# Experts' gated values turned four blocks at a time, kept in the place of the last norm's row

## The chip, the cores and the metric

The kernel runs on one core of one Trainium2 chip. The metric is the device time of one execution in microseconds; less is better. The core's engines are TensorE (PE; its weight loads PEld), VectorE (DVE), ScalarE (ACT), GpSimd (POOL) and SyncE (SP). Each runs its own instruction stream, and they meet at semaphores. A "q" behind an engine's name (PEldq, DVEq) is its sequencer: branches, waits, counts.

## What is computed

Two transformer blocks over 256 tokens of width 1024. The part that the change touches is the end of the second block: a mixture of experts (eight experts, two per token, 2816 hidden values) with the closing layer norm.

```python
def moe_swiglu(x, w_router, b_router, w_in, w_out):
    ...
    def expert_block(args):
        xb, e = args
        h = xb @ w_in[e]
        return (jax.nn.silu(h[:, :D_FF]) * h[:, D_FF:]) @ w_out[e]
...
def layer_norm(x, g, b):
    xf = x.astype(jnp.float32)
    mu = jnp.mean(xf, axis=-1, keepdims=True)
    var = jnp.mean(jnp.square(xf - mu), axis=-1, keepdims=True)
    return ((xf - mu) * lax.rsqrt(var + LN_EPS) * g + b).astype(x.dtype)
...
        x = layer_norm(DN_ALPHA * x + ffn, ln_ffn_g[i], ln_ffn_b[i])
```

## The kernel before

All engines run the same plan: first block, sparse feed-forward of the first block, first layer of the second block, second layer with the router, then the experts. The experts are one body (`expert`), run in a loop for experts 0 to 6, written out for expert 7, and written out three more times as overflow blocks (`OVER`), each in an `If` on a count from the router; where an expert has no more than 128 tokens the `Else` (`skip`) runs instead and only raises the semaphores by what the body would have raised (`each_expert`, L714). With the inputs used, all three overflow blocks are skipped.

One expert, for its 128 token slots: the weights stream through a ring of six units of 2 MB. 11 units are slabs of the up product ("up"; each gives 256 columns of each half), 7 are pieces of the output product ("y"). A unit is used in two halves ("pieces"). Each piece is split by ScalarE into a rounded part (`piece_hi`, four places, L1192) and by VectorE into the rest (`weights_low`, L2222), and TensorE multiplies hi*hi, hi*low and low*hi. The order in which TensorE works is the list `Y`, that of ScalarE and VectorE the list `E_SEQ` (L365 to L379).

Between up and y stand the gated values. ScalarE takes the silu of half a bank into `silu_e` (L1216), VectorE multiplies it by the other half into `gated` (L2258), which has two places in the scratch region; TensorE turns a slab's 128x256 values by two 128x128 transposes into a bank (L1632); ScalarE copies them rounded to `ge_hi` (L1192), VectorE subtracts to `ge_low` (L2234). This job is called ("ge", n), one for each of the 11 slabs, and stands in both lists behind slab n + 2. VectorE waits before it writes slab n's gated values until ("ge", n - 2) is turned. The tokens of the next expert are fetched by POOL with an indirect DMA into `tokens`, the first of two places of `rows` (L610, L868), and turned four blocks at a time (L1584).

`rows` has two places of 1024 values on all partitions. The norms' rows (g and b) are loaded into them in turn, even ones into place 0, odd ones into place 1 (`load_row`, L810 to L815). Of the last norm's two rows, b (`late_row + 1`, place 1) is loaded before the experts begin (L864), because place 1 is then free; g (`late_row`, place 0) is loaded after the last tokens are turned (L869, L870).

At the end VectorE adds each expert's sums to the tokens (L2272), goes through its three skips (L2280), and normalises tile 0, then tile 1 (`layer_norm_tile`, L1726): statistics, a multiplication by g (L1731), the root, the reciprocal (L1733), and two halves with b (L1736). SP writes the outputs by halves as they are ready (L801). `layer_norm_tile` waits for both rows ahead of L1731.

The semaphore `e_product` counts TensorE's jobs of the experts: it is raised by one at the end of each, and by a whole expert's number, `N_EP`, by TensorE's `skip`:

```python
        def skip(b):
            pe.wait_ge(e_product, b * N_EP + N_EP)
            pe.sem_inc(e_product, N_EP)
```

The other names that the diff touches: `E_BANK` gives each job its PSUM bank; `wait_split(..., e_low, what, ...)` waits until VectorE has the low part of `what`; `e_freed["vector"]` counts what VectorE has read or written.

Of the kernel before, what the change touches and what calls it, by code (L numbers as in the profile page):

```python
# [21 lines left out]
P = 128  # L22
S, D = 256, 1024
# [236 lines left out]
def two_blocks(nc, a):  # L260
# [101 lines left out]


    HIS = 4
    Y, E_SEQ = [], []  # L365
    for i in range(N_PIECE):
        Y.append(piece_end(i))
        n, more = i // 2, [("piece", i + HIS)] if i + HIS < N_PIECE else []
        turned = ("ge", n - 2) if i % 2 and 2 <= n < N_UP + 2 else None
        if i < 2 * N_UP and i % 2:  # L370
            E_SEQ += [("up", n), ("piece", i + HIS - 1)]
        if i >= 2 * N_UP or i % 2:
            E_SEQ += more
        if turned:
            Y.append(turned)
            E_SEQ.append(turned)
        if turned == ("ge", 1):
            Y.append(SLOTS)
            E_SEQ.append(SLOTS)  # L379
    E_ORDER = {False: Y[:-1] + GATHERED[:1] + Y[-1:] + GATHERED[1:] + SUMS + [("pickT", 0)], True: GATHERED + [("pickT", 0)] + Y + SUMS}  # L380
# [115 lines left out]
    top[0] = N_HI + 2 * FC * P + TILES * P + 2 * D  # L496
    pick = area(TILES * P, P)
    slot_gate = area(1)
    silu_e, gated = area(2 * S, S), area(2 * S, S)
    logits, r_mask, r_first, r_hot = (area(TILES * NE, NE) for _ in range(4))  # L500
    r_gate, r_slot = (area(TILES * (NE + 1), NE + 1) for _ in range(2))
    r_top, r_idx, r_idxf = area(TILES * 8, 8), area(TILES * 8, 8, U32), area(TILES * 8, 8)
# [164 lines left out]
    E_BANK = {("pickT", 0): 6, SLOTS: 7}  # L667
    for n in range(N_UP):
        E_BANK["up", n] = n % 4
        E_BANK["ge", n] = 4 + n % 2  # L670
    for n in range(N_SUM):
        E_BANK["sum", n] = n
    for h in range(HALVES):
# [131 lines left out]
    @block.gpsimd  # L805
    def _(pool):
        own = Own(pool, pool_step)
        pool.dma_start(pos_i, a["positions"][0].partition_broadcast(P)).then_inc(pos_in, 16)

        def load_row(i):  # L810
            if i >= 2:
                pool.wait_ge(row_used, i - 1)
            name = rows_order[i]
            src = a[name[0]][name[1]] if isinstance(name, tuple) else (a[name] if name == "g_final" else a[name][0])
            pool.dma_start(rows[:, i % 2, :], src.partition_broadcast(P)).then_inc(row_in[i % 2], 16)  # L815

        for i in range(2, 4):
            load_row(i)

        pool.wait_ge(product_ready, pl.nth["in", N_IN - 1])  # L820
        pool.dma_start(x_tok[:, :, :], a["x"][0].rearrange("(t p) n -> p t n", p=P)).then_inc(x_again, 16)
        pool.wait_ge(merged, KD)
        pool.dma_start(mem2T[:, :, :], a["mem_2_T"].rearrange("(k p) s -> p k s", p=P)).then_inc(mem2_in, 16)
        pool.dma_start(pos_i, a["positions_2"][0].partition_broadcast(P)).then_inc(pos_in, 16)


        def gather_u(s, k):
            if k == 0:
                pool.wait_ge(search_done, s + 1)
            pool.wait_ge(dots_done, s * TOPK + k + 1)  # L830
            pool.indirect_dma_start(u_ring[:, k % UV, :], None, a["peer_u"][0],  # L831
                                    bass.IndirectOffsetOnAxis(idx[:, s % IDX_SETS, k:k + 1], 0)).then_inc(u_in[k % UV], 16)

        def gather_v(s, k):
            n = s * TOPK + k
            if n < VV and n % (UNIT // D) == 0:
                pool.wait_ge(product_ready, pl.nth[V_FROM[n // (UNIT // D)]])
            if n < VV or by_pe(n - VV):
                pool.wait_ge(v_used, summed_to(n - VV))
            else:  # L840
                pool.wait_ge(v_added, ADDED.index(n - VV) + 1)
            pool.indirect_dma_start(v_row(n), None, a["peer_v"][0],  # L842
                                    bass.IndirectOffsetOnAxis(idx[:, s % IDX_SETS, k:k + 1], 0)).then_inc(v_in[n % VV], 16)

        def u_rows_ahead(n):
            return TOPK if n < UNIT // D else TOPK + 8 if n < 2 * UNIT // D else TOPK + 4

        gathered_u = 0
        for n in range(STEPS * TOPK):
            while gathered_u < min(n + 1 + u_rows_ahead(n), STEPS * TOPK):  # L850
                gather_u(gathered_u // TOPK, gathered_u % TOPK)
                gathered_u += 1
            gather_v(n // TOPK, n % TOPK)
        late_row = len(rows_order) - 2
        assert late_row % 2 == 0
        for i in range(4, late_row):
            load_row(i)
        pool.wait_ge(cum_ready, 1)
        for h in range(SH):
            row = other_half[h % 2].start  # L860
            pool.dma_start(kz[row:row + 1, h, :], f_cum[h:h + 1, :]).then_inc(decay_rows_in, 16)
        pool.wait_ge(normed, HALVES * TILES * 7)
        pool.dma_start(x_rows.rearrange("(t p) n -> p t n", p=P), x_tok[:, :, :]).then_inc(x_saved, 16)
        load_row(late_row + 1)  # L864
        pool.wait_ge(x_saved, 16)
        for b in range(NE - 1):
            pool.wait_ge(slots_ready, b + 1)
            pool.indirect_dma_start(tokens, None, x_rows, bass.IndirectOffsetOnAxis(slot_token[:, 0:1], 0)).then_inc(tokens_in, 16)  # L868
        pool.wait_ge(e_product, (NE - 1) * N_EP + e_at(GATHERED[-1], False) + 1)  # L869
        load_row(late_row)  # L870


    @block.scalar
    def _(act):
# [298 lines left out]
        def split(what, b, over):  # L1173

            kind, n = what
            if kind == "y":
                act.wait_ge(e_freed["scalar"], (b + 1 + over) * e_n["scalar"])
                act.activation(ye_hi[:, 512 * n:512 * n + 512], wait_e(what, b, over), ACT.Copy, scale=slot_gate).then_inc(e_hi, 1)
                return
            if kind == "gather":  # L1180
                src, dst = wait_e(what, b, over).rearrange("p (k s) -> p k s", k=4), xe_hi[:, 4 * n:4 * n + 4, :]
            elif kind == "ge":
                src, dst = wait_e(what, b, over)[:, 0:S].rearrange("p (f s) -> p f s", f=2), ge_hi[:, 2 * n:2 * n + 2, :]
            else:
                src, dst = piece(n), hi_of(n)
                if n % 2 == 0:
                    u = n // 2
                    turn = b if over or n >= HIS else b + 1
                    act.wait_ge(weight_in[u % RING], turn * per_expert[u % RING] + pl.loaded[u % RING] + e_loaded[u])
                if n >= HIS or not over:  # L1190
                    act.wait_ge(e_product, b * N_EP + N_EP + e_at(piece_end((n - HIS) % N_PIECE), over) + 1)
            act.activation(dst, src, ACT.Copy).then_inc(e_hi, 1)  # L1192
# [60 lines left out]
    def _(pe):  # L1253
# [355 lines left out]
        def expert(e, b, over):  # L1609
# [5 lines left out]
            for j in Y:  # L1615
# [11 lines left out]
                if j[0] == "ge":  # L1627
                    n = j[1]
                    bank = bank_of(j, b, over)
                    pe.wait_ge(e_freed["vector"], b * e_n["vector"] + e_n["vector"] + e_nth(("up", n), over))  # L1630
                    for f in range(2):
                        ins = pe.transpose(bank[:, f * P:(f + 1) * P], gated[:, n % 2, f * P:(f + 1) * P], ident)  # L1632
                    ins.then_inc(e_product, 1)
                    continue
                i = next(i for i in range(N_PIECE) if piece_end(i) == j)
# [12 lines left out]
                else:  # L1648
                    o, h = divmod(i - 2 * N_UP, HALVES)
                    bank = bank_of(("y", h), b, over) if o == 0 else psum[:, E_BANK["y", h], :]  # L1650
                    f0 = sum(OUT_ROWS[:o])
                    wait_split(pe, e_low, ("ge", (f0 + OUT_ROWS[o] - 1) // 2), b, over)
                    wait_split(pe, e_low, ("piece", i), b, over)
                    for k in range(OUT_ROWS[o]):
                        f = f0 + k
# [33 lines left out]
    def _(dve):  # L1689
# [36 lines left out]
        def layer_norm_tile(t, src):  # L1726

            own(dve.bn_aggr(mv[:, 2 * t:2 * t + 2], bn[:, 12 * t:12 * t + 12]))  # L1728
            tell(dve.tensor_scalar(stat[:, t:t + 1], mv[:, 2 * t + 1:2 * t + 2], LN_EPS, None, ALU.add), square_ready, n_square)  # L1729
            g, b = wait_row(dve, n_row[0]), wait_row(dve, n_row[0] + 1)  # L1730
            own(dve.scalar_tensor_tensor(x_tok[:, t, :], src[:, t, :], mv[:, 2 * t:2 * t + 1], g, ALU.subtract, ALU.mult))  # L1731
            dve.wait_ge(root_ready, n_square[0])
            own(dve.reciprocal(rstd[:, t:t + 1], rstd[:, t:t + 1]))  # L1733
            for h in range(HALVES):
# [482 lines left out]
        def split(what, b, over):  # L2217
# [12 lines left out]
            if kind == "gather":  # L2230
                bank, hi, low = psum[:, E_BANK[what], :].rearrange("p (k s) -> p k s", k=4), xe_hi[:, 4 * n:4 * n + 4, :], xe_low[:, 4 * n:4 * n + 4, :]
            else:
                bank, hi, low = psum[:, E_BANK[what], 0:S].rearrange("p (f s) -> p f s", f=2), ge_hi[:, 2 * n:2 * n + 2, :], ge_low[:, 2 * n:2 * n + 2, :]
            dve.tensor_tensor(low, bank, hi.bitcast(F32), ALU.subtract).then_inc(e_low, 1)  # L2234
            dve.wait_ge(e_low, b * N_SPLIT + N_SPLIT + E_SPLITS[over].index(what) + 1)
            dve.sem_inc(e_freed["vector"], 1)
# [1 line left out]
        def expert(e, b, over):  # L2238
# [4 lines left out]
            for j in E_SEQ:  # L2243
# [9 lines left out]
                    continue  # L2253
                n = j[1]
                dve.wait_ge(e_silu, b * N_UP + n + 1)
                if n >= 2:
                    wait_e(("ge", n - 2), b, over)
                dve.tensor_tensor(gated[:, n % 2, :], silu_e[:, n % 2, :], psum[:, E_BANK[j], S:2 * S], ALU.mult)\  # L2258
                   .then_inc(e_freed["vector"], 1)
            last = b == NE - 1 if isinstance(b, int) else False  # L2260
            for j in E_OUT if over else OPENING + CLOSING:
# [115 lines left out]
```

## Time and profile before

| | |
|---|---|
| median of 3 runs | 2350.22 us (2348.09 to 2350.32) |
| profiled execution, its own time | 2348.31 us |
| its span | 2346.3 us |
| TensorE busy | 2129.1 us, 91% |
| VectorE busy | 1563.8 us, 67% |
| ScalarE busy | 1069.1 us, 46% |
| POOL busy | 512.2 us, 22% |
| granted TensorE clock, mean | 0.990 |

The span goes from the first to the last instruction; the time of the execution has some 2 us more around it. The experts take about the last third of the span. In the rows further on, a time is counted from the start of the span; an instruction's duration on TensorE is longer than the distance to the next one, since products overlap.

### The profile page before, as it was taken

To read this page: it belongs to the slowest core of one execution; us is meant where nothing else is said; L and a number is where in the kernel's file an instruction comes from. 1 tells how busy PE (TensorE), PEld (TensorE's weight loads), DVE (VectorE), ACT (ScalarE), POOL (GpSimd) and SP (SyncE) were. 2 spreads that over 40 slices of the span, in tenths; PEclk is the share of its full clock that TensorE was granted. 3 is DMA by queue.
4 is the path that set the end of the run, shared out by engine and by line. 5 is a ranking of instruction groups with operands and counts; after the bars stand their busy time and mean duration, and the time that the engine had idled before them with its cause. 6 is when DMAs were issued, how large, how long until landed. Compare 5 with 4: busy or idle time off the path is not lost. (4 is left out here: it accounts for less than half of the span.)

```text
span 2346.3 us, 27245 instructions
## 1 busy us (share of the span) xinstructions
PE 2129.1 (91%) x9328; PEld 1529.5 (65%) x9328; DVE 1563.8 (67%) x2560; ACT 1069.1 (46%) x1565; POOL 512.2 (22%) x550
## 2 busy tenths in 40 slices
PE   7999999877777777789999999899999999999997
PEld 5998867322222222257599886578878788787875
DVE  5775338666666666544455432479888898888987
ACT  3496014221222212114444325367777777777764
POOL 0000007777777777610000010000000000000000
PEclk9999999999999999999999999999999999999998
DMA  8444429999999999994253643279999999999993
GB/s 309 159 156 180 163 92 378 404 410 409 409 409 409 409 410 409 409 351 160 90 180 135 242 162 108 99 241 318 363 344 355 350 360 362 344 359 350 357 363 136
DMA packets 356585, 683.41 MB, mean 291 GB/s; under 512 B 14016, under 2 KB 222016, under 8 KB 356352
## 3 DMA queue, kind: packets, MB, share of 16 engines
q1 hardware_dynamic: 279008, 401.24, 50.4%
q0 software_dynamic: 77472, 280.80, 30.2%
q8 instruction: 61, 1.00, 0.2%
q14 instruction: 44, 0.36, 0.0%
HBM read 679.88 MB, written 2.10 MB: 291 GB/s over the span
## 5 line engine op out<-in xcount | busy, mean ns | idle before, releaser
L2222 DVE TENSOR_TENSOR weights_low<-weight_ring,piece_hi 128x2048 fp32r<-128x2048 f32 (+1 forms) x286 | 590.1, 2109 | 48.6 <-ACT piece_hi L1192 42.7
L1440 PE MATMUL psum<-weight_ring,region 128*128 128x512 f32 x988 | 478.0, 609 | 142.8 <-DMA weight_ring<-in_peer_v,region 139.6
L1192 ACT ACTIVATE piece_hi<-weight_ring 128x2048 fp32r<-128x2048 f32 (+1 forms) x286 | 494.7, 1768 | 30.4 <-PE psum L1658 27.8
L1440 PEld LDWEIGHTS psum<-weight_ring,region 128*128 128x128 f32 x988 | 169.0, 189 | 451.4 <-issue 303.5
L2041 DVE CUSTOM_DVE_ANT_0 weight_ring<-weight_ring,psum 128x1024 f32<-128x1024 f32 x224 | 273.6, 1221 | 206.0 <-DMA weight_ring<-in_peer_u,region 206.0
L1645 PE MATMUL psum<-piece_hi,tokens_hi 128*128 128x512 f32 x704 | 284.7, 404 | 5.4 <-DVE weights_low L2222 2.7
L831 POOL DMA_INDIRECT weight_ring<-in_peer_u,region x256 | 248.0, 969 | 140.0 <-DVE region L2015 53.0
L1647 PE MATMUL psum<-piece_hi,tokens_low 128*128 128x512 f32 x704 | 277.8, 395 | 0.0
L1646 PE MATMUL psum<-weights_low,tokens_hi 128*128 128x512 f32 x704 | 277.7, 394 | 0.0
L842 POOL DMA_INDIRECT weight_ring<-in_peer_v,region x256 | 242.5, 947 | 90.7 <-issue 69.7
L1043 ACT ACTIVATE region<-constants,region 128x128 f32<-128x128 f32 x247 | 88.3, 395 | 284.6 <-PE psum L1440 209.6
L1291 PE MATMUL psum<-actT,weight_ring 128*128 128x256 f32 x720 | 161.5, 384 | 1.8 <-DMA weight_ring<-in_w_mem_kv 1.8
L1645 PEld LDWEIGHTS psum<-piece_hi,tokens_hi 128*128 128x128 f32 x704 | 132.6, 188 | 36.7 <-DVE weights_low L2222 5.8
L1647 PEld LDWEIGHTS psum<-piece_hi,tokens_low 128*128 128x128 f32 x704 | 132.5, 188 | 31.2
L1291 PEld LDWEIGHTS psum<-actT,weight_ring 128*128 128x128 f32 x720 | 138.4, 193 | 21.8 <-DMA weight_ring<-in_w_mem_kv 2.2
L1646 PEld LDWEIGHTS psum<-weights_low,tokens_hi 128*128 128x128 f32 x704 | 132.8, 189 | 27.8
L868 POOL DMA_INDIRECT rows<-x_rows,region x7 | 6.6, 946 | 641.6 <-DVE region L2247 641.6
L1656 PE MATMUL psum<-piece_hi,gated_hi 128*128 128x512 f32 x352 | 140.3, 399 | 0.3 <-PEq L1570 0.3
L1658 PE MATMUL psum<-piece_hi,gated_low 128*128 128x512 f32 x352 | 137.6, 391 | 0.0
L1657 PE MATMUL psum<-weights_low,gated_hi 128*128 128x512 f32 x352 | 137.1, 389 | 0.0
L890 ACT ACTIVATE region<-psum 128x256 f32<-128x256 f32 (+2 forms) x119 | 56.1, 475 | 173.9 <-PE psum L1291 89.2
L2123 DVE TENSOR_TENSOR ring_low<-weight_ring,ring_hi 128x2048 fp32r<-128x2048 f32 (+1 forms) x36 | 76.0, 2114 | 58.5 <-ACT ring_hi L1085 58.5
(313 smaller groups left out, 3434.0 us busy)
## 6 DMA issues: line engine op xcount, KB each, us to landing
weight_ring<-in_w_exp_in SPq DMA_DIRECT2D x176, 1024.0 KB, 11.8
weight_ring<-in_w_exp_out SPq DMA_DIRECT2D x48, 1536.0 KB, 9.3
weight_ring<-in_w_in SPq DMA_DIRECT2D x12, 2048.0 KB, 7.8
weight_ring<-in_w_ffn_in SPq DMA_DIRECT2D x22, 1024.0 KB, 7.7
weight_ring<-in_w_exp_out SPq DMA_DIRECT2D x8, 2048.0 KB, 8.9
weight_ring<-in_w_out SPq DMA_DIRECT2D x6, 2048.0 KB, 8.4
weight_ring<-in_w_in_fox SPq DMA_DIRECT2D x5, 2048.0 KB, 7.9
weight_ring<-in_w_ffn_out SPq DMA_DIRECT2D x6, 1536.0 KB, 6.7
```

Of the source, the lines that this page charges most:

```text
L831: pool.indirect_dma_start(u_ring[:, k % UV, :], None, a["peer_u"][0], bass.IndirectOffsetOnAxis(idx[:, s % IDX_SETS, k:k + 1], 0)).then_in ...
L842: pool.indirect_dma_start(v_row(n), None, a["peer_v"][0], bass.IndirectOffsetOnAxis(idx[:, s % IDX_SETS, k:k + 1], 0)).then_inc(v_in[n % V ...
L1192: act.activation(dst, src, ACT.Copy).then_inc(e_hi, 1)
L1291: ins = pe.matmul(bank[:, 0:S], w[:, k, c * P:(c + 1) * P], src[:, k, :], start=(k == 0), stop=(k == nk - 1))
L1440: ins = pe.matmul(psum[:, peer_bank(t, half), :], diag[:, k, :], v_row(n)[:, 512 * half:512 * half + 512], start=(s < TILES and k == 0), s ...
L1645: pe.matmul(bank, xe_hi[:, k, :], h_, start=(k == 0), stop=False)
L1646: pe.matmul(bank, xe_hi[:, k, :], l_, start=False, stop=False)
L1647: ins = pe.matmul(bank, xe_low[:, k, :], h_, start=False, stop=(k == KD - 1))
L1656: pe.matmul(bank, ge_hi[:, f, :], hi[:, k, :], start=(f == 0), stop=False)
L1658: ins = pe.matmul(bank, ge_low[:, f, :], hi[:, k, :], start=False, stop=(f == FC - 1))
L2041: dve.tensor_tensor_reduce(u_ring[:, k % UV, :], u_ring[:, k % UV, :], h2, 1.0, 0.0, ALU.mult, ALU.add, u_dot[:, t, k:k + 1]).then_inc(dot ...
L2222: dve.tensor_tensor(low_of(n), piece(n), hi_of(n).bitcast(F32), ALU.subtract).then_inc(e_low, 1)
```

## The change

`ge` jobs become fewer and larger: job q turns slabs 2q and 2q + 1 with four transposes into one bank; the last one has the single slab 10. There are six (`N_TURN`). Job q stands behind slab 2q + 3, the last behind slab 12 of the list (the second unit of the output product), where ("ge", 10) stood. The copy to `ge_hi` and the subtraction to `ge_low` take 512 columns at once. `gated` gets four places instead of two, and these are place 1 of `rows`. So row b of the last norm can't be loaded ahead of the experts: POOL loads it after all experts and overflow blocks are counted in `e_product`. `layer_norm_tile` waits for b only after the multiplication by g.

```diff
     HIS = 4
+    N_TURN = -(-N_UP // 2)
+    TURNED_AT = {2 * q + 3: ("ge", q) for q in range(N_TURN - 1)}
+    TURNED_AT[N_UP + 1] = ("ge", N_TURN - 1)
+    units_turned = lambda q: range(2 * q, min(2 * q + 2, N_UP))
...
-        turned = ("ge", n - 2) if i % 2 and 2 <= n < N_UP + 2 else None
+        turned = TURNED_AT.get(n) if i % 2 else None
...
-        if turned == ("ge", 1):
+        if turned == ("ge", 0):
...
-    silu_e, gated = area(2 * S, S), area(2 * S, S)
+    silu_e = area(2 * S, S)
+    gated = rows[:, 1, :].rearrange("p (u s) -> p u s", u=4)
...
-        E_BANK["ge", n] = 4 + n % 2
+    for q in range(N_TURN):
+        E_BANK["ge", q] = 4 + q % 2
...
         pool.dma_start(x_rows.rearrange("(t p) n -> p t n", p=P), x_tok[:, :, :]).then_inc(x_saved, 16)
-        load_row(late_row + 1)
+        pool.wait_ge(row_used, late_row)
         pool.wait_ge(x_saved, 16)
...
         pool.wait_ge(e_product, (NE - 1) * N_EP + e_at(GATHERED[-1], False) + 1)
         load_row(late_row)
+        pool.wait_ge(e_product, (NE + OVER + 1) * N_EP)
+        load_row(late_row + 1)
...
-                src, dst = wait_e(what, b, over)[:, 0:S].rearrange("p (f s) -> p f s", f=2), ge_hi[:, 2 * n:2 * n + 2, :]
+                f0, nf = 4 * n, 2 * len(units_turned(n))
+                src, dst = wait_e(what, b, over)[:, 0:nf * P].rearrange("p (f s) -> p f s", f=nf), ge_hi[:, f0:f0 + nf, :]
...
-                    pe.wait_ge(e_freed["vector"], b * e_n["vector"] + e_n["vector"] + e_nth(("up", n), over))
-                    for f in range(2):
-                        ins = pe.transpose(bank[:, f * P:(f + 1) * P], gated[:, n % 2, f * P:(f + 1) * P], ident)
+                    pe.wait_ge(e_freed["vector"], b * e_n["vector"] + e_n["vector"] + e_nth(("up", units_turned(n)[-1]), over))
+                    for u in units_turned(n):
+                        for f in range(2):
+                            at = (2 * (u % 2) + f) * P
+                            ins = pe.transpose(bank[:, at:at + P], gated[:, u % 4, f * P:(f + 1) * P], ident)
...
-            g, b = wait_row(dve, n_row[0]), wait_row(dve, n_row[0] + 1)
+            g = wait_row(dve, n_row[0])
             own(dve.scalar_tensor_tensor(x_tok[:, t, :], src[:, t, :], mv[:, 2 * t:2 * t + 1], g, ALU.subtract, ALU.mult))
+            b = wait_row(dve, n_row[0] + 1)
...
-                if n >= 2:
-                    wait_e(("ge", n - 2), b, over)
-                dve.tensor_tensor(gated[:, n % 2, :], silu_e[:, n % 2, :], psum[:, E_BANK[j], S:2 * S], ALU.mult)\
+                if n >= 4:
+                    wait_e(("ge", (n - 4) // 2), b, over)
+                dve.tensor_tensor(gated[:, n % 4, :], silu_e[:, n % 2, :], psum[:, E_BANK[j], S:2 * S], ALU.mult)\
```

## Rows read from the trace of the kernel before

**Rows 1.** Busy time by stretch: us, then PE, PEld, DVE, ACT, POOL, clock, DMA.

```profile
1600.00:2200.00 600.00, 595.60 (x2688) 482.00 (x2688) 533.67 (x431) 436.35 (x395) 5.64 (x6) 1.00 1.05 353
2300.00:2346.00 46.00, 29.04 (x127) 22.77 (x125) 33.24 (x36) 18.29 (x17) 0.00 (x0) 0.86 0.24 85
```

**Rows 2.** Waits, 1600 to 2200: waiting line, releaser, us in total, times, longest.

```profile
PEld psum L1645 <- DVE weights_low L2222: 4.9, 6, 0.8
PEld psum L1668 <- DVE out_low L2225: 3.8, 6, 0.6
```

**Rows 3.** Groups by form, 1600 to 2200: busy us, mean ns, idle before.

```profile
L2234 DVE TENSOR_TENSOR gated_low<-psum,gated_hi 128x256 fp32r<-128x256 f32 x67 | 28.1, 419 | 0.0
L1192 ACT ACTIVATE gated_hi<-psum 128x256 fp32r<-128x256 f32 x67 | 24.8, 371 | 0.0
L2234 DVE TENSOR_TENSOR tokens_low<-psum,tokens_hi 128x512 fp32r<-128x512 f32 x12 | 8.3, 692 | 2.7 <-DVE out_low L2225 2.7
L1192 ACT ACTIVATE tokens_hi<-psum 128x512 fp32r<-128x512 f32 x12 | 7.1, 590 | 0.0
```

**Rows 4.** Timeline of TensorE around a turn of two: start, us.

```profile
1699.93 0.39 PE L1647 MATMUL psum<-piece_hi,tokens_low 128*128 128x512 f32 x1
1700.16 0.38 PE L1632 MATMUL psum<-constants,region 128*128 128x128 f32 x2
1700.30 0.48 PE L1656 MATMUL psum<-piece_hi,gated_hi 128*128 128x512 f32 x1
1700.61 0.40 PE L1657 MATMUL psum<-weights_low,gated_hi 128*128 128x512 f32 x1
```

**Rows 5.** Timeline of TensorE around a turn of four (tokens).

```profile
1728.18 0.60 PE L1584 MATMUL psum<-constants,rows 128*128 128x128 f32 x4
1728.54 0.48 PE L1656 MATMUL psum<-piece_hi,gated_hi 128*128 128x512 f32 x1
1728.85 0.40 PE L1657 MATMUL psum<-weights_low,gated_hi 128*128 128x512 f32 x1
```

**Rows 6.** Timeline: two low parts, and the product that needs the first.

```profile
1784.50 4.49 DVE L2222 TENSOR_TENSOR weights_low<-weight_ring,piece_hi 128x2048 fp32r<-128x2048 f32 x2 [0.23 <-ACT piece_hi L1192]
...
1787.93 0.48 PE L1645 MATMUL psum<-piece_hi,tokens_hi 128*128 128x512 f32 x1
```

**Rows 7.** Lines L723 and L1678: ns min/median/max, first and last start.

```profile
L723 ACTq COMPARE_BRANCH  x3: 45/45/50, 2328.1 to 2331.2; - x3
L723 PEldq COMPARE_BRANCH  x3: 3899/5022/5420, 2330.1 to 2339.4; - x3
...
L1678 PEldq EVENT_SEMAPHORE  x3: 51/51/51, 2334.0 to 2344.9; - x3
```

**Rows 8.** Timeline: POOL's load of row g, and what released it.

```profile
2227.28 0.60 PE L1584 MATMUL psum<-constants,rows 128*128 128x128 f32 x4
...
2228.18 0.57 POOL L815 DMA_DIRECT2D rows<-in_ln_ffn_g  x1 [64.25 <-PE psum L1584]
```

**Rows 9.** Lines L815 (at 1358, at 2228) and L801: the issues, us to landing.

```profile
L815 POOL DMA_DIRECT2D rows<-in_ln_attn_g x1: 528/528/528, 1358.5 to 1358.5; - x1
DMA to landing us min/median/max: 3.7/3.7/3.7
...
L815 POOL DMA_DIRECT2D rows<-in_ln_ffn_g x1: 567/567/567, 2228.2 to 2228.2; - x1
DMA to landing us min/median/max: 6.6/6.6/6.6
...
L801 SPq DMA_DIRECT2D out<-x_tok x4: 332/342/360, 2338.4 to 2343.8; - x4
DMA to landing us min/median/max: 2.0/2.0/5.4
```

**Rows 10.** The tail: VectorE's timeline in tile 0, POOL's drain (ns).

```profile
2336.14 1.29 DVE L1731 SCALAR_TENSOR_TENSOR x_tok<-work_tok,small,rows 128x1024 f32<-128x1024 f32 x1
2337.46 0.16 DVE L1733 RECIPROCAL small<-small 128x1 f32<-128x1 f32 x1
...
L2314 POOLq DRAIN  x1: 10397/10397/10397, 2228.2 to 2228.2; - x1
```

More of the change, by code:

```diff
@@ L854, in _ @@
         late_row = len(rows_order) - 2
-        assert late_row % 2 == 0
         for i in range(4, late_row):
@@ L1651, in expert @@
                     f0 = sum(OUT_ROWS[:o])
-                    wait_split(pe, e_low, ("ge", (f0 + OUT_ROWS[o] - 1) // 2), b, over)
+                    wait_split(pe, e_low, ("ge", (f0 + OUT_ROWS[o] - 1) // 4), b, over)
                     wait_split(pe, e_low, ("piece", i), b, over)
@@ L2232, in split @@
             else:
-                bank, hi, low = psum[:, E_BANK[what], 0:S].rearrange("p (f s) -> p f s", f=2), ge_hi[:, 2 * n:2 * n + 2, :], ge_low[:, 2 * n:2 * n + 2, :]
+                f0, nf = 4 * n, 2 * len(units_turned(n))
+                bank, hi, low = psum[:, E_BANK[what], 0:nf * P].rearrange("p (f s) -> p f s", f=nf), ge_hi[:, f0:f0 + nf, :], ge_low[:, f0:f0 + nf, :]
             dve.tensor_tensor(low, bank, hi.bitcast(F32), ALU.subtract).then_inc(e_low, 1)
```

## Prediction

> **What bounds the kernel now.** I read the busy time by stretch first. From 1600 to 2200 us, inside the expert loop, TensorE is busy 595.6 of 600 us, VectorE 533.7, ScalarE 436.4, all at full granted clock [rows 1]. So the loop is TensorE's, and work taken from ScalarE or VectorE is worth only what TensorE waits for them. The waits of the same stretch say how much: 4.9 us for the weights' low part, six times, once per expert, and 3.8 us for the output's low part [rows 2]. Both lie at the joint between two experts (the first up product of the third slab, and the four sums), not at a turn of gated values.
>
> The last 46 us look different: TensorE is busy 29 us of 46 [rows 1]. What ends last there is VectorE's closing layer norm and the outputs behind it. I then asked for the lines that look idle: what each sequencer does there. TensorE passes three skipped overflow blocks. Each skip is a branch over the body of an expert and takes 3.9, 5.0 and 5.4 us, and the count that tells of a skip (L1678) follows each: the first at 2334.0, the last at 2344.9 [rows 7]. Nobody waits for those counts in the kernel before; the span ends 1.35 us after the last one.
>
> **The change part by part.**
>
> *Turns in TensorE.* Before, 11 groups of two transposes per expert; after, five groups of four and one of two. The number of transposes stays 22. What a group of two costs: from its first start, 1700.16, to the second product behind it, 1700.61, is 0.45 us; one ordinary product of that kind takes 0.23 (1699.93 to 1700.16), so 0.22 for the pair [rows 4]. The same for a group of four, read where gathered tokens are turned: 1728.18 to 1728.85 is 0.67, less 0.23 gives 0.44 [rows 5]. Four cost twice two: a transpose costs 0.11 us and the grouping itself nothing. Gain on TensorE: 0. The bounds: below, a saving if the second pair rode free, 5 x 8 x 0.22 = 8.8 us; the row of four excludes it nearly.
>
> *The rounding copy on ScalarE and the subtraction on VectorE.* Per merged pair VectorE goes from 2 x 419 to 692 ns and ScalarE from 2 x 371 to 590 (the 128x512 forms are those of the gathered tokens) [rows 3]: some 0.15 us each, 40 merged pairs, 6 us on each engine. All of it lies under TensorE. The 4.9 us of waits by the third slab are not touched, because in the order of an expert that piece comes ahead of the first turn. Gain taken: 0.
>
> *Later and longer pieces of work in order.* The longer subtraction (692 for 419, 0.27 us more) now stands before the next slab's low part. Before, the low parts of the slab that starts at 1787.93 begin at 1784.50 and, at half of 4.49 us, the first is ready at 1786.75: 1.2 us of slack [rows 6]. It covers 0.27; and summed from the start of an expert, VectorE and ScalarE have never more to do than before (nothing after slab 3 of one pair, then one long form where two short ones stood). Without that cover it would be 40 x 0.27 = 10.9 us.
>
> *Waits for the gated buffer.* Four places instead of two: VectorE waits for a turn two slabs old rather than for the one just made. Less waiting, on an engine with slack: 0.
>
> *The row of the last norm, taken away from 1515.* One POOL issue and 512 KB less beside the weights, 50 us ahead of POOL's next need. Nobody waited for it: 0.
>
> *The layer norm's order.* The wait for row b moves behind the multiplication by g. It is a sequencer wait during a 1.29 us instruction: 0. It does let tile 0 do its first pass before b is there.
>
> *The row of the last norm, loaded at the end.* This is where the time goes. POOL waits until every product of eight experts and three overflow blocks is counted. That count is TensorE's third skip, not its last product. Behind the wait on POOL stands the load alone; on the load waits VectorE, in order, with the rest of tile 0 and all of tile 1. Step by step:
> - release: 2344.9 plus the 0.05 of the count itself: 2344.95 [rows 7];
> - POOL's answer: the other row's load starts at 2228.18, after four transposes that started at 2227.28 and took 0.60, so 0.30 us: issue at 2345.25 [rows 8];
> - landing: 3.7 us for such a row at 1358.5, 6.6 at 2228.2 among the experts' weights [rows 9]. At the end no weights move, so I take 3.7; the 256 KB outputs, half as large and on the other queue, land in 2.0, my lower end [rows 9]. Row there at 2348.95;
> - VectorE resumes with the reciprocal, which began at 2337.46 before [rows 10]. With 0.1 us to take up the wait (an estimate, twice the 0.05 of a sequencer wait) it begins at 2349.05: 11.6 us later. All behind it (tile 0's second pass, tile 1, the outputs) keeps its length, 8.8 us to the end of the span.
> Sum: +11.6 us on the profiled execution, 2346.3 us of span and 2348.31 with what lies around it, so 2359.9. That execution stands with the lower of the runs shown (2348.09); the median shown is 2350.22. Of the four numbers the middle is 2349.3, and I give 2349.3 + 11.6 = 2360.9.
>
> Where a second wait could hide: POOL's closing drain took 10.4 us from the load's issue [rows 10]. From 2345.25 that gives 2355.6, ahead of VectorE's and the outputs' new end at 2357.8. It is covered by 2 us.
>
> The unknown is how long the three branches take after the change, since the body they jump over has a few instructions less. Bounds by the rows: all three like the shortest, 11.7 us instead of 14.3, or all like the longest, 16.2: -2.6 to +1.9.
>
> One rule speaks against this sum. The Trainium skill, Advanced Engine Details and Errata, section "Control Flow Timing", gives a compare-and-branch about 108 ns. By it the three skips would be over by 2330.3 or so and the row would cost nothing; the trace shows 3.9 to 5.4 us instead. The Trainium skill, Runtime: NRT & Kernel Launch, section "Instruction fetch mechanics", says that a taken branch to a target outside the fetched window stalls for a fetch of it; that agrees with the trace's order of size and gives no number.
>
> **The rivals.**
> - *The skips release early and the row is hidden* (not slower). If TensorE's branches were short, the row would be needed only at 2337.46; back by 4.1 us (0.30 + 3.7 + 0.1) it must be released by 2333.4. The skips are all counted by then only if they took under 3.4 us together. For it: ScalarE's records of the same branches are 0.05 us long [rows 7]. Against it: the three rows of 3.9 to 5.4 us. Time: 2349.3. Chance 0.04. The control-flow figure cited above would give this case.
> - *Groups cost, not transposes.* The second pair rides free: -8.8, together with the late row 2352.1. Against it rows 5. Chance 0.04.
> - *The long form eats the slack.* 40 x 0.27 us on top: 2360.9 + 10.9 = 2371.8. It decides where slack falls under 0.27; it is 1.2 in the row read, smaller at an expert's start where no turn stands. Chance 0.04.
> - *The row lands slowly or the branches lengthen.* 6.6 instead of 3.7: 2363.8; with the longest branches 2365.7. Chance 0.13, partly inside my range by intent.
>
> **How the numbers follow.** Forecast with its sizes (landing 2.0 to 4.5, branches as before or up to 2.6 shorter): 0.75. Range: lower end, 2360.9 less 1.7 (landing) and less 2.6 (branches), 2356.6, and half a microsecond for the spread of the runs: 2356. Upper end: 2365.7, rounded to 2366. Outside lie the first three rivals, 0.12, and a little of the sizes. A measurement of this kernel tells about 0.2%, 4.7 us, from no change. Slower by more: 0.75 + 0.13 + 0.04 = 0.92. Within: the early release and the free pairs, 0.08, of which I move 0.01 to faster, for 0.07 and 0.01.
>
> **What would show it.** In the profile after: the load of the last row on POOL at about 2345, after L1678's third count; VectorE idle for about 11.6 us ahead of the reciprocal of tile 0, with a DMA or POOL as its releaser; TensorE busy time from 1600 to 2200 unchanged within 1 us; six turn groups per expert with a pitch of 0.11; 512-wide forms of 590 and 692 ns. Wrong would be: the load well before 2340, a wait of VectorE that stands elsewhere, TensorE waits by a turn's low part, or POOL's drain as the last to end.

## The result and the profile after

| | before | changed |
|---|---|---|
| median, 7 runs each | 2350.65 us | 2357.32 us (2356.6 to 2360.3) |
| ratio | | 1.0036 (95%: 1.0027 to 1.0045), +8.5 us (6.3 to 10.6) |
| again, on another chip (19 and 5 runs) | 2349.90 us | 2359.23 us, ratio 1.0040 (1.0026 to 1.0053), +9.4 us |
| profiled execution | 2348.31 us, span 2346.3 | 2356.77 us, span 2354.7 |
| start of TensorE's last product | 2329.5 | 2327.5 |
| from there to the end of the span: the closing part | 16.8 us | 27.2 us |

The kernel became slower, and the closing part is where the profile shows it. The ratio on record is 1.0036; the two medians of the first row lie 6.7 us apart, less than the 8.5 us of the ratio but inside its interval. Differences below are the ratio times the median of the kernel before. Line numbers have moved: L1632 is now L1642, L2234 L2246, L1678 L1688, L723 L729, L815 L821, L1733 L1744.

The expert loop first, in the same three views as before: the waits of TensorE from 1600 to 2200, the groups by form in the same stretch, and its busy time (us, then PE, PEld, DVE, ACT, POOL, clock, DMA):

```profile
PEld psum L1655 <- DVE weights_low L2233: 4.9, 6, 0.8
PEld psum L1678 <- DVE out_low L2236: 3.8, 6, 0.6
```

```profile
L2246 DVE TENSOR_TENSOR gated_low<-psum,gated_hi 128x512 fp32r<-128x512 f32 x30 | 20.5, 684 | 0.0
L1200 ACT ACTIVATE gated_hi<-psum 128x512 fp32r<-128x512 f32 x30 | 17.6, 586 | 0.0
L2246 DVE TENSOR_TENSOR gated_low<-psum,gated_hi 128x256 fp32r<-128x256 f32 x6 | 2.5, 417 | 0.0
```

```profile
1600.00:2200.00 600.00, 595.62 (x2688) 483.02 (x2688) 530.29 (x400) 435.83 (x364) 5.64 (x6) 1.00 1.05 354
```

They stand against rows 1 to 3. The two waits have not moved by a tenth. The merged forms are there, 30 in six experts' time, and VectorE is busy 3.4 us less in 600; TensorE is busy as before (595.62 us for 595.60). A group of four turns in place:

```profile
1691.88 0.40 PE L1657 MATMUL psum<-piece_hi,tokens_low 128*128 128x512 f32 x1
1692.12 0.60 PE L1642 MATMUL psum<-constants,rows 128*128 128x128 f32 x4
1692.47 0.47 PE L1655 MATMUL psum<-piece_hi,tokens_hi 128*128 128x512 f32 x1
1692.78 0.39 PE L1656 MATMUL psum<-weights_low,tokens_hi 128*128 128x512 f32 x1
```

From the first turn, 1692.12, to the second product behind it, 1692.78, are 0.66 us. Less one product's 0.23 that is 0.43 for four turns, twice the 0.22 of the pair in rows 4.

Now the end. First TensorE's counts and branches, L1688 and L729 (ns, first and last start), then lines of the timeline from VectorE's pass with g to its reciprocal:

```profile
L1688 PEldq EVENT_SEMAPHORE  x3: 51/51/51, 2331.6 to 2341.6; - x3
...
  POOL rows L821: 115.1, 1
...
L729 PEldq COMPARE_BRANCH  x3: 3362/4551/4992, 2328.1 to 2336.5; - x3
```

```profile
2334.93 1.27 DVE L1741 SCALAR_TENSOR_TENSOR x_tok<-work_tok,small,rows 128x1024 f32<-128x1024 f32 x1
...
2341.90 0.55 POOL L821 DMA_DIRECT2D rows<-in_ln_ffn_b  x1 [115.10 <-PEq L1688]
2345.90 0.16 DVE L1744 RECIPROCAL small<-small 128x1 f32<-128x1 f32 x1 [9.69 <-DMA rows<-in_ln_ffn_b]
```

POOL's load now waits for the third count, at 2341.6. The load starts at 2341.90, lands 3.9 us later, and VectorE, which finished the pass with g at 2336.2, waits 9.69 us for it. From the reciprocal to the end of the span are 8.8 us, as in rows 10.

### The profile page after: what moved, and what is told of

Its sections match the earlier page's. It is cut to its first block and busy times, and to the rows that moved or that the text cites. A ratio compares the mean times of both kernels' runs of the same rounds, so it can differ in the third digit from the quotient of the medians.

```text
span 2354.7 us, 26985 instructions
## 1 busy us (share of the span) xinstructions
PE 2127.3 (90%) x9328; PEld 1529.2 (65%) x9328; DVE 1557.4 (66%) x2520; ACT 1066.8 (45%) x1525; POOL 513.6 (22%) x550
```

## The experiments

Each kernel ran beside the kernel before on its chip. The first four ran on a chip where every kernel takes 66 us longer, all of it ahead of the experts (the kernel before: 2415.76, at a mean granted clock of 0.959 to 0.969, for 0.986 to 0.992 on the others); the experts' part is as long there. Lengths of the closing part are from the start of TensorE's last product to the end of the span. Differences in us against the kernel before are the ratio times its median, with the 95% interval.

### The turns without the row

```diff
@@ gpsimd, changed kernel
-        pool.wait_ge(e_product, (NE + OVER + 1) * N_EP)
-        load_row(late_row + 1)
@@ layer_norm_tile
-            b = wait_row(dve, n_row[0] + 1)
+            b = g if n_row[0] + 2 == len(rows_order) else wait_row(dve, n_row[0] + 1)
```

This kernel leaves out row b of the last norm and adds g in its place; its operations keep their sizes.

> The changed kernel without the load of the last norm's row b; the norm uses row g in its place (the output's last norm is therefore another one; everything else is computed). It keeps the turns of four blocks, the four places, the later wait. Theory A (the late row is the only cost, the turns are worth nothing, the profiled pair's 2.1 us ahead of the experts is scatter): as the kernel before, within 1 us of it; span about 2346. Rival B (the turns, or what they displace, give something back that the late row hides): 2 to 4 us faster than the kernel before. Rival C (the turns cost): slower by 1 us or more.

Measured: ratio 1.0004 (0.9995 to 1.0012), +1.0 us (-1.2 to 2.9); closing part 18.0 us. Rival B, that the turns give back 2 to 4 us, falls. A small cost isn't excluded. In the closing part VectorE's idle time ahead of its statistics has grown. The line of the kernel before, and that of this one:

```profile
2334.36 1.42 DVE L1724 BATCH_NORM_STATS2 small<-work_tok 128x6 f32<-128x512 f32 x2 [2.94 <-DVEq L2287]
```

```profile
2402.78 1.42 DVE L1732 BATCH_NORM_STATS2 small<-work_tok 128x6 f32<-128x512 f32 x2 [3.54 <-DVEq L2297]
```

That is VectorE's own way through the three skips: 3.5 to 3.7 us idle in six profiles with the turns in which no row is in flight then, 2.94 and 2.45 in the two profiles of the old body. Of the 1.2 us that this run's closing part is longer, 0.6 lie there; the other 0.6 lie behind the reciprocal, where its outputs took 2.7 to 4.3 us to land, for a median of 2.0 before.

### The row without the turns

```diff
@@ gpsimd, kernel before
-        load_row(late_row + 1)
+        pool.wait_ge(row_used, late_row)
...
         load_row(late_row)
+        pool.wait_ge(e_product, (NE + OVER + 1) * N_EP)
+        load_row(late_row + 1)
@@ layer_norm_tile: the wait for b behind the multiplication by g, as in the change
```

> The kernel before with the last norm's row b loaded at the end as in the changed one (after TensorE's third skip), and the wait for b behind the multiplication by g; turns of two blocks, two places, as before. Theory A: slower than the kernel before by as much as the changed kernel's closing part is longer, 10 us (16.7 us from the last sum to the end in the profile before, 27.1 in the one after), less what the branches vary, so +8 to +11, and not different from the changed kernel by more than 1 us. Rival B: slower than the changed kernel by the 2 to 4 us that the turns give back.

Measured: ratio 1.0048 (1.0036 to 1.0060), +11.6 us (8.7 to 14.5); closing part 27.9 us. The late row without the turns costs as much as the whole change does or more, so it accounts for all of the loss. The theory had said +8 to +11.

```profile
2399.77 1.42 DVE L1726 BATCH_NORM_STATS2 small<-work_tok 128x6 f32<-128x512 f32 x2 [2.45 <-DVEq L2290]
2409.94 0.56 POOL L815 DMA_DIRECT2D rows<-in_ln_ffn_b  x1 [115.25 <-PEq L1680]
2414.52 0.16 DVE L1736 RECIPROCAL small<-small 128x1 f32<-128x1 f32 x1 [11.71 <-DMA rows<-in_ln_ffn_b]
```

### Another release of the row

```diff
@@ gpsimd, changed kernel
-        pool.wait_ge(e_product, (NE + OVER + 1) * N_EP)
+        pool.wait_ge(e_freed["vector"], (NE + OVER + 1) * e_n["vector"])
         load_row(late_row + 1)
```

This is the release by VectorE's count; by ScalarE's the new line is

```diff
+        pool.wait_ge(e_hi, (NE + OVER + 1) * N_SPLIT)
```

Both counts are full only when every turn of gated values has been made, so place 1 is free then too.

> The changed kernel, but POOL waits for the count of what VectorE has read in all experts and overflow blocks, instead of TensorE's. In the profile after, VectorE's third skip is counted at 2333.1, TensorE's at 2341.6. Theory A (the third skip of TensorE releases the row): 8.5 us less wait; the row lands 0.34 + 3.9 us after 2333.1, at 2337.4, where the reciprocal could begin at 2336.3: so 8 to 9 us faster than the changed kernel and about 1 us slower than the kernel before. Rival D (the row's transfer, or POOL, is what takes the time at the end, not the release): no more than 2 us faster than the changed kernel.

> The changed kernel, but POOL waits for ScalarE's count of splits, whose third skip is counted at 2329.4 in the profile after. Theory A: the row lands at 2329.4 + 4.2 = 2333.6, ahead of the reciprocal at 2336.3, so nothing is left of its cost: as the kernel before within 1 us, 9 to 10 us faster than the changed one. Rival B as in the first run: 2 to 4 us faster than the kernel before. Rival D: no more than 2 us faster than the changed kernel.

> The fourth run's kernel again, beside the kernels of this call. Theory A: the row costs nothing. Theory E (what was left there, 1.7 us of the closing part, is VectorE's third skip, which is counted 0.6 to 1.5 us later than before, and not the row): between +0.5 and +2.5 us over the kernel before, with the row landed by 6.6 us after the last sum and the reciprocal at 8.5 to 9.5.

Measured, by VectorE: +1.9 us (-0.2 to 4.3), closing part 19.0. By ScalarE: +2.9 (1.0 to 5.1) and, on a third chip, +1.4 (-0.7 to 3.5), closing parts 18.4 and 18.3.

```profile
2401.49 0.55 POOL L821 DMA_DIRECT2D rows<-in_ln_ffn_b  x1 [106.29 <-DVEq L2299]
2406.14 0.16 DVE L1744 RECIPROCAL small<-small 128x1 f32<-128x1 f32 x1 [1.81 <-DMA rows<-in_ln_ffn_b]
```

```profile
2398.40 0.55 POOL L821 DMA_DIRECT2D rows<-in_ln_ffn_b  x1 [102.61 <-ACTq L1248]
2402.80 1.42 DVE L1734 BATCH_NORM_STATS2 small<-work_tok 128x6 f32<-128x512 f32 x2 [4.42 <-DVEq L2299]
2405.88 0.17 DVE L1744 RECIPROCAL small<-small 128x1 f32<-128x1 f32 x1
```

Rival D, the transfer or POOL as the cost, falls: the same load, asked for 9 to 13 us sooner, costs 1.4 to 2.9 us instead of 8.5 to 11.6. By VectorE's count the reciprocal still waits 1.81 us for the row; by ScalarE's it waits for nothing (the row is there 4.6 us after 2398.40), and yet 1.6 us of the closing part stay. They lie ahead of the statistics, which start 1.5 us later than in the kernel before: VectorE's skips now take 4.42 us of idle time (4.52 when repeated), against 3.5 to 3.7 with the turns where no row is in flight, and 2.94 before. So theory A's zero was wrong for this kernel (its interval, 1.0 to 5.1, excludes it), and theory E holds for the place.

### The changed kernel again, and both rows awaited first

```diff
@@ layer_norm_tile, changed kernel
-            g = wait_row(dve, n_row[0])
+            g, b = wait_row(dve, n_row[0]), wait_row(dve, n_row[0] + 1)
             own(dve.scalar_tensor_tensor(x_tok[:, t, :], src[:, t, :], mv[:, 2 * t:2 * t + 1], g, ALU.subtract, ALU.mult))
-            b = wait_row(dve, n_row[0] + 1)
```

> The changed kernel itself, beside the kernel before on the same chip as the next three runs. Theory A (the tail alone, 10.4 us longer in the profiled pair, is the effect; 6.7 us between the medians is that less scatter of the earlier stages): +9 to +12 over the kernel before, 27 us from the last sum to the end. Rival B (something ahead of the tail gives back 2 to 4 us): +6 to +8 again.

> The changed kernel, but the norm waits for both rows before the multiplication by g, as the kernel before does. Theory A (VectorE is held in order by the late row): the multiplication, 1.28 us, moves behind the landing, so 1.3 us slower than the changed kernel on this chip; 28.4 us from the last sum to the end. If the wait for the row were not what holds the end, no difference.

Measured: the changed kernel +9.4 us (6.1 to 12.5), closing part 28.1. The interval holds the +9 to +12 of theory A and also the +6 to +8 of rival B; what speaks against B is the first run, not this one. With both rows first the median doesn't differ, 2359.10 against 2359.23, closing part 28.8. The median doesn't show the 1.3 us; the profile does, once the release is taken out:

```profile
2345.18 0.55 POOL L821 DMA_DIRECT2D rows<-in_ln_ffn_b  x1 [115.64 <-PEq L1688]
2349.48 0.16 DVE L1744 RECIPROCAL small<-small 128x1 f32<-128x1 f32 x1 [10.71 <-DMA rows<-in_ln_ffn_b]
```

```profile
2342.72 0.55 POOL L821 DMA_DIRECT2D rows<-in_ln_ffn_b  x1 [114.75 <-PEq L1688]
2348.67 0.16 DVE L1743 RECIPROCAL small<-small 128x1 f32<-128x1 f32 x1
```

From issue to reciprocal: 4.30 us, against 5.95 with both rows first, 1.65 more (1.28 of it the pass with g, 0.3 a slower landing, 4.5 for 4.2). But the load came 14.05 us after the last product instead of 14.96: in that one execution the branches were quicker. An effect of 1.3 us is inside the scatter of the branches.

### One overflow block

```diff
-    OVER = 3
-    assert (OVER + 1) * (P + 1) > 2 * S
+    OVER = 1
```

With one block the result is right as long as no more than one expert has over 128 tokens, as with these inputs. The seventh expectation says "over 256 tokens", which no expert can have with 256 tokens in all.

> The kernel before with one overflow block instead of three (the two left out are not needed by these inputs; an expert with over 256 tokens would be wrong). Theory A: VectorE's statistics follow the first skip, at about 2.0 us after the last sum instead of 4.85; 2.8 us faster than the kernel before; 13.9 us from the last sum to the end.

> The changed kernel with one overflow block instead of three. Theory A (the row is released by TensorE's last skip): the only skip is counted 4.1 us after the last sum, the row lands at 4.1 + 0.34 + 3.9 = 8.3, the reciprocal starts at 8.4, and the end is 8.7 later, 17.1: about 10 us faster than the changed kernel, within 1 us of the kernel before, and 3.2 us slower than the seventh run. Rival D (the load itself or POOL is the cost): no more than 3 us faster than the changed kernel.

Measured: the kernel before with one block -5.2 us (-7.5 to -2.8), closing part 14.1; the changed one -2.1 (-4.2 to 0.0), closing part 18.3.

```profile
L1687 PEldq EVENT_SEMAPHORE  x1: 51/51/51, 2334.5 to 2334.5; - x1
...
2334.82 0.56 POOL L820 DMA_DIRECT2D rows<-in_ln_ffn_b  x1 [104.46 <-PEq L1687]
2339.53 0.16 DVE L1743 RECIPROCAL small<-small 128x1 f32<-128x1 f32 x1 [4.26 <-DMA rows<-in_ln_ffn_b]
```

With two branches of TensorE gone the change costs 3.9 us between the two medians (2347.56 and 2343.68) and 4.2 us of closing part, instead of 9.3 and 11: the loss goes with the number of skips. That is the strongest evidence for the release. The expectation said 3.2; the landing took 4.6 instead of 3.9. The kernel before gained more than the 2.8 us forecast, 5.2: 2.7 in the closing part, and 0.9 at the joint ahead of expert 7. That wait of 1.02 us stands there, within 0.01, in five profiles with three blocks, nested or not, and in neither of the two with one. The engines read the blocks' counts there, three instead of one, which I take for the reason. The rest, 1.6 us, I can't place. First the kernel before, then with one block:

```profile
2230.25 0.50 PE L1606 MATMUL psum<-region 128*128 128x1 f32 x4
2231.78 0.47 PE L1645 MATMUL psum<-piece_hi,tokens_hi 128*128 128x512 f32 x1 [1.02 <-DVE work_tok L2272]
```

```profile
2228.54 0.50 PE L1605 MATMUL psum<-region 128*128 128x1 f32 x4
2229.16 0.47 PE L1644 MATMUL psum<-piece_hi,tokens_hi 128*128 128x512 f32 x1
```

### The row loaded twice

```diff
@@ gpsimd, changed kernel
         load_row(late_row + 1)
+        pool.wait_ge(row_in[1], 16 * ((late_row + 1) // 2))
+        load_row(late_row + 1)
@@ layer_norm_tile: the last norm waits for the second load
```

> The changed kernel, with the last norm's row b loaded a second time after the first load has landed; the norm waits for the second. Theory A (issue and landing lie whole on the path): the closing part grows by one more landing, 4.3 us (3.9 to 4.6 in the profiles so far), and POOL's answer, 0.3: +4.6 us over the changed kernel, so about +14 over the kernel before; 32 us from the last sum to the end. If another wait (POOL's drain, the outputs) held the end, less than 2 us more.

Measured: +17.1 us (13.6 to 20.9) against the kernel before, closing part 31.9, 3.9 more than in the changed kernel's second profile and 4.8 more than in its first; the expectation was +4.6 and about +14. The landing lies whole on the path, and POOL's drain does not hold the end. The closing part is 15.1 us longer than before; the 17.1 between the runs is more, from four runs, and its interval holds both numbers.

```profile
2344.92 0.55 POOL L821 DMA_DIRECT2D rows<-in_ln_ffn_b  x1 [115.25 <-PEq L1690]
2349.12 0.53 POOL L821 DMA_DIRECT2D rows<-in_ln_ffn_b  x1 [3.65 <-DMA rows<-in_ln_ffn_b]
2353.13 0.16 DVE L1750 RECIPROCAL small<-small 128x1 f32<-128x1 f32 x1 [14.28 <-DMA rows<-in_ln_ffn_b]
```

### Nested overflow blocks

```diff
-        for i in range(OVER):
+        def overflow(i):
             with eng.If(counts[i] > P):
                 body(eng.value_load(over_e[0:1, i:i + 1], min_val=0, max_val=NE - 1), i + NE, True)
+                if i + 1 < OVER:
+                    overflow(i + 1)
             with eng.Else():
-                skip(i + NE)
+                for k in range(i, OVER):
+                    skip(k + NE)
+        overflow(0)
```

> The kernel before with the three overflow blocks nested: the second stands inside the first, the third inside the second, so that one branch skips all three (the counts come sorted, so the result is the same for all inputs). Theory A on the skips: VectorE passes one branch instead of three, statistics at about 2.1 us after the last sum instead of 4.85, the end at 14.1 instead of 16.7: 2.6 us faster than the kernel before. The joint ahead of expert 7 stays, so less than the 6.2 us of the run with one block.

> The changed kernel with the overflow blocks nested and the row released by ScalarE's count. That count is full before the last sum (ScalarE's one branch follows its last split), so POOL issues the row at about 0, it lands by 4.5, and the reciprocal could begin at 5.2: no cost. Theory A and E: as the eleventh run within 1 us, 2 to 3 us faster than the kernel before and 11 to 13 us faster than the changed one. Rival B would make it 2 to 4 us faster than the eleventh run.

Measured: -0.7 us (-2.8 to 1.4), closing part 17.3; with the turns and ScalarE's release 0.0 (-2.1 to 2.1), closing part 17.0. The expectation of 2.6 us failed in the profile: the one branch over three bodies leaves VectorE idle longer than three branches did (3.43 us, for 2.94). The median's interval alone, down to -2.8, would not exclude it.

```profile
L723 PEldq COMPARE_BRANCH  x1: 3849/3849/3849, 2331.0 to 2331.0; - x1
...
L1683 PEldq EVENT_SEMAPHORE  x3: 51/51/51, 2334.9 to 2335.2; - x3
...
2335.76 1.42 DVE L1729 BATCH_NORM_STATS2 small<-work_tok 128x6 f32<-128x512 f32 x2 [3.43 <-DVEq L2292]
```

TensorE gains by the nest. It passes it with a single branch of 3.8 us (3.5 with the turns), which is within the 3.4 to 5.4 us of a branch over one body, and all three counts are up 4.8 us after its last product (2330.42), instead of 13.7 to 15.4. So its time goes by the number of branches here, not by how many bodies one jumps over. The changed kernel with the blocks nested and TensorE's own count as the release was not run. As an estimate from these rows, its load would start at 5.1 us and land by 9.0 to 9.9, for a reciprocal at 8.4: most of the loss would be gone by nesting alone.

The last kernel has the whole change and costs nothing that could be measured, but doesn't beat the kernel before. No kernel with three overflow blocks did.

## Why the prediction was right, step by step

The forecast was +11.6 us, 2360.9, from 2356 to 2366; measured are 2357.3, and +8.5 (6.3 to 10.6) and +9.4 (6.1 to 12.5) in two comparisons. The side and the mechanism were right, and each link of the mechanism was shown: the release by the count of TensorE's third skip (one overflow block, the other releases), the landing (the row twice), the late row as the part that costs (the two halves of the change alone).

The size was less well met than the total. The added 11.6 us lie above the first interval, 6.3 to 10.6, and inside the second. The total came nearer, 3.6 us too high, because the base that I chose, 2349.3, was 1.4 us below the median of all seven runs, 2350.65: that is luck.

| term | forecast | measured |
|---|---|---|
| turns in TensorE, gain | 0 | waits and busy time as before; the turns alone +1.0 (-1.2 to 2.9) |
| longer forms on ScalarE, VectorE | covered | covered, 684 and 586 ns, no new wait of TensorE |
| third count, after the last product | 15.4 (2344.9, rows 7) | 14.1 and 14.6 in the changed kernel's two profiles |
| POOL's answer | 0.30 | 0.25 from the end of the count at 2341.65 |
| landing | 3.7 | 3.9 and 4.2 there; 3.9 to 4.8 in eight others |
| reciprocal to the end | 8.8 | 8.8 |
| closing part, in all | 16.8 + 11.6 | 27.2 and 28.1: +10.4 and +11.3 |

*The branches were the mis-sized term of the closing part.* I took them from one execution. With the old body in another profile (the row without the turns) the third count comes at 14.2 us, and in all nine other profiles with three separate skips between 13.7 and 14.6. The 15.4 of the profile before is the largest of ten. So nothing shows that the change shortened the branches, though two profiles of the old body are few: the profile before had long ones, and the forecast was 0.8 to 1.3 us too high for it, inside the -2.6 to +1.9 that had been set aside.

*The landing was too short* by 0.2 and 0.5 us in the changed kernel's two profiles, which gave a part back. The loads of this row at the end took 3.9 to 4.8 in ten profiles; none came down to the 3.7 of rows 9.

*The base.* In the profile after the last product starts 2.0 us earlier than in the one before. That isn't the change's. The two POOL queues differ first at the load that stood behind the tokens' store, and that store already starts 2.0 us earlier:

```profile
1514.44 0.75 POOL L863 DMA_DIRECT2D x_rows<-x_tok  x1 [127.88 <-DVE x_tok L1736]
```

```profile
1512.41 0.75 POOL L868 DMA_DIRECT2D x_rows<-x_tok  x1 [127.84 <-DVE x_tok L1747]
```

In the changed kernel's second profile the last product starts 0.7 us later (2330.22). The stages ahead of the experts scatter by this much.

*What stays open.* The closing part grew by 10.4 and 11.3 us in profiles; the comparisons of medians say 8.5 and 9.4. Each interval holds the profile's number of its pair, but a gain of 1 to 2 us elsewhere would not be seen in them. The turns alone give no sign of one.

*The rivals.* The early release (no cost) did not happen by itself; made by hand, with ScalarE's or VectorE's count, it cost 1.4 to 2.9 us where that rival had nothing. Free pairs: not so, 0.43 us for four turns. Slack eaten by the long form: no new wait. POOL's drain, the second wait that I had set aside at 10.4 us, took 8.0 in the profile after and ended at 2349.9, ahead of VectorE; in no run was it last.

## What to carry to other kernels

A buffer's new place has to be priced by who can free it at the end of the program, not by its size: one 512 KB row moved behind the last count cost 8.5 to 11.6 us in three comparisons, while all that it made room for was hidden by a busy TensorE. Before a wait is hung on a count, look when that count is really raised on the engine that raises it, its skips and branches included, and choose the earliest count that implies the same; here ScalarE's was full 12 us before TensorE's. Taking branches off that engine's way is the other means: one skip for three left 4.2 us of the loss. Here, merging small operations of engines that have slack gave nothing, as the bound engine's own number of operations stayed.

## What the hardware showed that I had not expected

A branch that skips an expert's body holds TensorE's sequencer for 3.4 to 5.4 us (ten profiles), though no product is left to do. On ScalarE the records of the same branches are 0.05 us long. The Trainium skill, Advanced Engine Details and Errata, section "Control Flow Timing", gives a compare-and-branch about 108 ns; for TensorE here the trace shows over thirty times that.

VectorE passes the same three skips with 2.5 to 3.7 us of idle time, and with 4.4 and 4.5 in the two profiles in which the 512 KB row was in flight meanwhile. The Trainium skill, Runtime: NRT & Kernel Launch, section "Instruction fetch mechanics", says that a taken branch to a target outside the fetched window stalls for a DMA fetch. The section gives no time, so its agreement with the trace in the order of size, which the prediction claims, can't be checked. But the trace records such fetches. From 2327 to 2342 in the profile after, while TensorE and VectorE pass their skips, two DMA queues of instructions moved five packets each, of 16 KB and of 8 KB, and no other queue moved anything:

```profile
q8 instruction: 5, 0.08, 3.4%
q14 instruction: 5, 0.04, 1.0%
```

They also place the microsecond. VectorE's third branch starts 3.1 us after the last product in the profile after and in the one with ScalarE's release (2330.6 and 2399.6):

```profile
L729 DVEq COMPARE_BRANCH  x3: 56/56/63, 2328.2 to 2330.6; - x3
```

```profile
L729 DVEq COMPARE_BRANCH  x3: 56/56/63, 2397.1 to 2399.6; - x3
```

In the profile after, a packet of q14 lies in the 0.9 us around and behind it (2330.53 to 2331.43). With ScalarE's release the same stretch (2399.47 to 2400.37) holds only the row's packets, on q0, and the packet of q14 comes in the next one (to 2401.27), between more of the row's:

```profile
q14 instruction: 1, 0.01, 3.8%
```

```profile
q0 software_dynamic: 54, 0.22, 65.6%
```

```profile
q0 software_dynamic: 61, 0.22, 88.2%
q14 instruction: 1, 0.01, 2.4%
```

The repeat of this run shows the same, and all six profiles with the turns and no row in flight show the early packet. So a fetch that the row's transfer holds up fits the 4.4 and 4.5. It fits the nested blocks too, where VectorE was idle for 3.2 us with the row and 3.4 without: their only branch was taken at 2329.7 and the row was asked for at 2331.23, and no packet of q14 stands where the row moves (2332.05 to 2333.85). That VectorE waited for this packet is inferred from the times; the trace does not say for whom it was.

POOL's closing drain starts with the issue of its last load and ends about 4 us after the landing: 8.0 to 8.5 us in the ten profiles that load the row at the end, 10.4 in the one before, among the weights, where the landing took 6.6.

```profile
L2326 POOLq DRAIN  x1: 8002/8002/8002, 2341.9 to 2341.9; - x1
```
